# Squares of three norms summed by a matrix of ones onto all partitions, in place of column sums and diagonals

## The chip, the cores and the metric

The kernel runs on one core of a Trainium2 chip. The metric is the device time of one execution in microseconds (us), median of several runs.

## The reference

One inference step of a hybrid causal decoder trunk with two layers, for 1024 prompt positions and 8 x 8 sample positions (1088 tokens together), model width 1024, all in float32. What matters for the change are the norms:

```
def _rmsnorm(x, g):
    y = x * rsqrt(mean(x * x) + EPS);  return y * g
def _layernorm(x, g, b):
    xc = x - mean(x);  return xc * rsqrt(mean(xc * xc) + EPS) * g + b

for i in range(2):
    xn = rmsnorm(x, norm_mix_g[i]);  z = xn @ w_in[i]
    ...                              # branches a, c, d
    glu = z_cfa * sigmoid(z_cfb);  yb = causal_depthwise_conv31(glu)
    br_b = silu(layernorm(yb + bias, ln_g, ln_b))        # 256 channels
    mixed = sum over branches of sigmoid(z_gate) * (branch @ w_branch)
    x = x + mixed @ w_out[i]
    xn = rmsnorm(x, norm_ffn_g[i])
    x = x + (dense swiglu if i == 0 else top-2-of-8 swiglu experts)(xn)
    g = sigmoid(rmsnorm(x, norm_ple_g[i]) @ ple_w_gate[i])
    x = x + g * (p[i] @ ple_w_proj[i])
y = rmsnorm(x, final_norm_g)
```

## The kernel before

Activations lie transposed: channels on the 128 partitions (8 groups of 128 for the width 1024), the 1088 tokens along the free axis, cut into three BLOCKS of 384, 384 and 320. Every float32 product is made of three fast ones: weights and activations are split into a high and a low half (WHI and WLO, XHI and XLO), and `product` (L699) runs high x high, low x high, high x low for 8 groups, 24 matmuls into one bank. `column_unit` (L720) does this for one 128-column piece of a weight and the three blocks. Weights stream from HBM into WRAW (two buffers); ScalarE writes WHI (`convert`, L1278, with gains multiplied in first for some tiles, L1290) and VectorE writes WLO (L1703), about three units ahead of TensorE.

TensorE has eight PSUM banks: six (BANKS) for the products, taken in turn by `open_bank`, which waits until VectorE has read the bank of six before; and banks 6 and 7, taken in turn by `misc_bank` (L693) for sums, transposes and small products. `misc_bank` waits until the last use but one has been freed (semaphore misc_free, counted up by VectorE). The order of work on every engine is written out by hand: each engine runs its own program, a helper may be given a function `between`, run behind block 0 or 1 of a unit, and the engines meet in semaphores.

The gains of a norm are in the weights and its mean or root is applied after the product, as a factor per token, RSTD, of 128 equal rows (L1824, L2232). It comes about so:

1. the squares of all channels are added up to SQS (128 partitions x 1088 tokens), or SQB (two channel groups) in the layer norm;
2. `token_sums` (L726): per tile of 128 tokens a matmul with the squares as weights and one column of ones as data gives the sums with the tokens on the partitions, 128 x 9 numbers;
3. `norm_tokens` (L1740): VectorE copies these 9 columns to RTOK, ScalarE takes the root (`norm_sqrt`, L1317), VectorE the reciprocal (L1746);
4. `diagonals` (L1749): VectorE multiplies the identity by each column into T, 128 x 1088;
5. `spread` (L739): TensorE multiplies T by the matrix ONES, which puts each token's factor on all partitions; VectorE copies it to RSTD (`spread_rstd`, L1762), or multiplies YB by it (L2131) in the layer norm.

The order around the places of the change, before it:

- **Layer norm of the convolution branch** (both layers). TensorE runs one column unit, with the sums of YB over channels behind its block 0 (`channel_sums`, L923, already with the matrix of ones); then `token_sums(SQB)`; then a second column unit with `spread` behind block 0; then `gate_project("br_b")`, with `states_out` (L794: transposes of the pool branch's state, L803 and L807) behind its first block, and the branch products L754 to L756 behind its third. VectorE: subtracts the mean (L2115), squares (L2117), takes the first unit's products (L1878), then steps 3 to 5, then YB goes to ScalarE for Silu (L1441, L1442) and the high half (L1341), back for the low half (L1805), a WLO conversion, the second unit's products (L1878), and the copies that `states_out` needs (L1889).
- **Feed-forward norm** (layer 0). The first unit of the feed-forward has `stats` (= `token_sums(SQS)`) behind block 0 and `spread` behind block 1. VectorE, after step 5, fills ACC (L2223) and goes on with the products.
- **First embedding norm** (layer 0). The first block of `gate_project("p_ready")` is followed by the transposes of p (`p_columns`, L856) and `stats`, the second by `spread`. Behind the third stand the branch products, which also wait for the low half of their weights (PWL, `split_pw`, L1793), made by VectorE after step 5.

Of the kernel before, what the change touches and what calls it, by code (L numbers as in the profile page):

```python
# [138 lines left out]
def build(nc, A, O):  # L139
# [106 lines left out]
    def mo(name, shape, dt=F32):  # L246
# [85 lines left out]
        "xnew_ready", "y_full", "v_out", "par_ready", "rw_loaded", "nrs_loaded", "rtok_clear", "row_squares", "scale_ready", "ids_ready", "mask_ready", "list_ready", "rows_written", "squared", "summed", "sums_taken", "weights_ready", "spacer")}  # L332
# [347 lines left out]
    def _(pe):  # L680
# [53 lines left out]

        def stats():
            pe.wait_ge(S["sq_ready"], sq.take())
            token_sums(SQS)
# [109 lines left out]
        for l in range(DEPTH):  # L847
# [75 lines left out]
            def channel_sums():  # L923
                pe.wait_ge(S["yb_ready"], l + 1)
                for t0, n in BLOCKS:
                    b = misc_bank()
                    for k in range(2):
                        ins = pe.matmul(PS[:, b, 0:n], ONES[:], YB[:, k, t0:t0 + n], start=(k == 0), stop=(k == 1))
                    ins.then_inc(m.next(), 1)

            column_unit(XHI, XLO, between=(channel_sums,))
            pe.wait_ge(S["lnsq_ready"], l + 1)
            token_sums(SQB[:, 0, :], SQB[:, 1, :])
            column_unit(XHI, XLO, between=(spread,))
# [14 lines left out]
            if l == 0:  # L949
                hs = Count()  # L950

                def step(kind, g, first=False):
                    if kind == "GU":
                        for u in range(4):
                            if first and u == 0:
                                column_unit(XHI, XLO, splits=lambda j, k: W_FFN - 3 * KC + 3 * k + j + 1, between=(stats, spread))
# [294 lines left out]
            if l == 0:  # L1251
                last_down = W_FFN + 6 * FFN_GROUPS
                gate_project("p_ready", 1, P_SPLIT[0], splits=lambda j, k: last_down + 3 * k + j + 1,
                             between=(lambda: (p_columns([PTOK[:, i, :] for i in range(NT)]), stats()), spread))
# [17 lines left out]
    def _(act):  # L1272
# [44 lines left out]
        def norm_sqrt(count=D):  # L1317
            serve(lambda: act.activation(RTOK[:], RTOK[:], ACT.Sqrt, bias=EPSC[:], scale=1.0 / count))

# [80 lines left out]
        for l in range(DEPTH):  # L1400
# [35 lines left out]
            plain(1)  # L1436
            norm_sqrt(DB)
            plain(1)
            m.n += 1 + 3
# [24 lines left out]
            m.n += 1  # L1464
            norm_sqrt()
            if l == 0:
                m.n += 3
# [161 lines left out]
            if l == 0:  # L1629
                split_branch(PTS[0], P_SPLIT[0])  # L1630
                m.n += 6 + 1
            norm_sqrt()
            m.n += 3
# [57 lines left out]
    def _(dve):  # L1691
# [77 lines left out]
        def norm_rows():  # L1769
# [4 lines left out]
            v.sync()  # L1774

# [178 lines left out]
        for l in range(DEPTH):  # L1954
# [265 lines left out]
            if l == 0:  # L2220
                norm()
# [436 lines left out]
```

## Time and profile before

| | |
|---|---|
| Median of 3 runs | 5056.26 us (5048.07 to 5062.81) |
| Span of the profiled execution | 5055.9 us (its own time isn't given beside it) |
| Mean granted TensorE clock | 0.987 of full speed |
| Busy: TensorE, VectorE, ScalarE, GpSimd | 4935.7, 3231.2, 1745.1, 302.4 us |
| Share of the chain that ended last | TensorE 81%, no wait shown 9%, VectorE 5%, DMA 2%, ScalarE 1% |

Busy time is the time in which an engine runs instructions; PE is TensorE, PEld its weight loads, DVE VectorE, ACT ScalarE, POOL GpSimd. Matmuls are pipelined: a row's duration overlaps the next, so the distance from start to start tells what one costs. One float32 matmul stands as two records. The chain that ended last is followed back from the last instruction to what released it.

### The profile page before, as it was taken

To read this page: it belongs to the slowest core of one execution; us is meant where nothing else is said; L and a number is where in the kernel's file an instruction comes from. 1 tells how busy PE (TensorE), PEld (TensorE's weight loads), DVE (VectorE), ACT (ScalarE), POOL (GpSimd) and SP (SyncE) were. 2 spreads that over 40 slices of the span, in tenths; PEclk is the share of its full clock that TensorE was granted. 3 is DMA by queue.
4 is the path that set the end of the run, shared out by engine and by line. 5 is a ranking of instruction groups with operands and counts; after the bars stand their busy time and mean duration, and the time that the engine had idled before them with its cause. 6 is when DMAs were issued, how large, how long until landed. Compare 5 with 4: busy or idle time off the path is not lost.

```text
span 5055.9 us, 87486 instructions
## 1 busy us (share of the span) xinstructions
PE 4935.7 (98%) x33281; PEld 4878.9 (96%) x33282; DVE 3231.2 (64%) x5248; ACT 1745.1 (35%) x2666; POOL 302.4 (6%) x441
## 2 busy tenths in 40 slices
PE   8999999999999999999979999999999999999998
PEld 8999999999998999999979999999999999999988
DVE  4666656444546656766557777666667787876655
ACT  3323322111113433233234444333334444443333
POOL 2000002111112000000020000000000000000030
PEclk9999999999999999999989999999999999999999
DMA  3111111111111111111025554444446555554431
GB/s 107 45 47 41 42 39 42 51 41 41 50 42 44 42 46 52 48 41 42 30 90 197 178 178 165 157 141 161 153 150 197 188 194 186 197 192 153 142 134 43
DMA packets 397853, 521.94 MB, mean 103 GB/s; under 512 B 13192, under 2 KB 353654, under 8 KB 397512
## 3 DMA queue, kind: packets, MB, share of 16 engines
q1 hardware_dynamic: 358320, 459.63, 27.5%
q10 hardware_dynamic: 29272, 33.08, 1.9%
q0 software_dynamic: 9920, 24.85, 1.7%
q8 instruction: 193, 3.16, 0.3%
q14 instruction: 148, 1.21, 0.1%
HBM read 494.91 MB, written 22.60 MB: 102 GB/s over the span
## 4 chain that ended last, share of the span: by engine, by line
PE 81%; issue 9%; DVE 5%; DMA 2%; ACT 1%; DVEq 0%; POOL 0%; ACTq 0%; SPq 0%; POOLq 0%
PE PS L705 20%; PE PS L707 19%; PE PS L706 19%; PE PS L818 5%; PE PS L820 5%; PE PS L819 5%; PE PS L754 1%; PE PS L755 1%; PE PS L756 1%; DMA WRAW<-in_moe_w_gate 1%; DVE EACC L2509 1%; PE PS L1244 1%; DVE WLO L1703 1%; ACT WHI L1302 1%; DVE XSL L2458 0%
## 5 line engine op out<-in xcount | busy, mean ns | idle before, releaser
L1703 DVE TENSOR_TENSOR WLO<-WRAW,WHI 128x1024 fp32r<-128x1024 f32 x866 | 1060.0, 1225 | 417.9 <-ACT WHI L1302 298.3
L705 PE MATMUL PS<-XHI,WHI 128*128 128x384 f32 (+1 forms) x3648 | 1200.9, 329 | 14.4 <-DVE XLO L1960 8.3
L707 PE MATMUL PS<-XHI,WLO 128*128 128x384 f32 (+1 forms) x3648 | 1196.1, 328 | 0.0
L1302 ACT ACTIVATE WHI<-WRAW 128x1024 fp32r<-128x1024 f32 x866 | 899.3, 1051 | 858.8 <-PE PS L820 603.4
L706 PE MATMUL PS<-XLO,WHI 128*128 128x384 f32 (+1 forms) x3648 | 1195.2, 328 | 0.0
L705 PE MATMUL PS<-XSH,WHI 128*128 128x232 f32 (+6 forms) x3584 | 1059.1, 296 | 14.5 <-DVEq L2461 12.0
L707 PE MATMUL PS<-XSH,WLO 128*128 128x232 f32 (+6 forms) x3584 | 1055.6, 295 | 0.0
L706 PE MATMUL PS<-XSL,WHI 128*128 128x232 f32 (+6 forms) x3584 | 1054.1, 294 | 0.0
L705 PEld LDWEIGHTS PS<-XHI,WHI 128*128 128x128 f32 x3648 | 689.9, 189 | 16.6 <-issue 9.0
L705 PEld LDWEIGHTS PS<-XSH,WHI 128*128 128x128 f32 x3584 | 678.8, 189 | 16.6 <-DVEq L2461 13.6
L706 PEld LDWEIGHTS PS<-XLO,WHI 128*128 128x128 f32 x3648 | 689.7, 189 | 0.9
L707 PEld LDWEIGHTS PS<-XHI,WLO 128*128 128x128 f32 x3648 | 689.4, 189 | 0.0
L707 PEld LDWEIGHTS PS<-XSH,WLO 128*128 128x128 f32 x3584 | 679.0, 189 | 0.0
L706 PEld LDWEIGHTS PS<-XSL,WHI 128*128 128x128 f32 x3584 | 678.7, 189 | 0.0
L818 PE MATMUL PS<-EHI,WHI 128*128 128x232 f32 (+6 forms) x1792 | 532.0, 297 | 4.8 <-DVE EACC L2509 3.0
L820 PE MATMUL PS<-EHI,WLO 128*128 128x232 f32 (+6 forms) x1792 | 525.0, 293 | 0.0
L819 PE MATMUL PS<-ELO,WHI 128*128 128x232 f32 (+6 forms) x1792 | 524.5, 293 | 0.0
L2509 DVE TENSOR_TENSOR EACC<-PS,EACC 128x336 f32<-128x336 f32 x832 | 372.7, 499 | 43.1 <-PE PS L820 15.9
L818 PEld LDWEIGHTS PS<-EHI,WHI 128*128 128x128 f32 x1792 | 338.8, 189 | 7.2 <-DVE EACC L2509 3.8
L1346 ACT ACTIVATE T<-T 128x384 f32<-128x384 f32 (+1 forms) x240 | 121.9, 508 | 640.7 <-DVEq L1826 640.4
L819 PEld LDWEIGHTS PS<-ELO,WHI 128*128 128x128 f32 x1792 | 338.9, 189 | 0.0
L820 PEld LDWEIGHTS PS<-EHI,WLO 128*128 128x128 f32 x1792 | 338.8, 189 | 0.0
(408 smaller groups left out, 5810.6 us busy)
## 6 DMA issues: line engine op xcount, KB each, us to landing
WRAW<-in_moe_w_gate SPq DMA_DIRECT2D x112, 1024.0 KB, 5.0
WRAW<-in_moe_w_up SPq DMA_DIRECT2D x112, 1024.0 KB, 5.0
WRAW<-in_moe_w_down SPq DMA_DIRECT2D x112, 1024.0 KB, 4.9
WRAW<-in_w_in SPq DMA_DIRECT2D x48, 1024.0 KB, 5.2
WRAW<-in_ffn_w_gate SPq DMA_DIRECT2D x11, 1024.0 KB, 5.3
WRAW<-in_ffn_w_up SPq DMA_DIRECT2D x11, 1024.0 KB, 5.3
WRAW<-in_ffn_w_down SPq DMA_DIRECT2D x11, 1024.0 KB, 4.9
expert_rows<-YT ACTq DMA_DIRECT2D x18, 512.0 KB, 3.8
```

The lines of the kernel that those rows point to most:

```text
L705: pe.matmul(PS[:, bank, 0:n], wh, hi(k), start=(k == 0), stop=False)
L706: pe.matmul(PS[:, bank, 0:n], wh, lo(k), start=False, stop=False)
L707: ins = pe.matmul(PS[:, bank, 0:n], wl, hi(k), start=False, stop=(k == KC - 1))
L754: pe.matmul(PS[:, b, 0:n], wh[:, k, :], Y[0][:, k, t0:t0 + n], start=(k == 0), stop=False)
L755: pe.matmul(PS[:, b, 0:n], wh[:, k, :], Y[1][:, k, t0:t0 + n], start=False, stop=False)
L818: pe.matmul(PS[:, b, 0:n], WHI[s][:, d, :], hi[:, f, t0:t0 + n], start=(f == 0), stop=False)
L819: pe.matmul(PS[:, b, 0:n], WHI[s][:, d, :], lo[:, f, t0:t0 + n], start=False, stop=False)
L820: ins = pe.matmul(PS[:, b, 0:n], WLO[s][:, d, :], hi[:, f, t0:t0 + n], start=False, stop=(f == 1))
L1302: act.activation(WHI[halves.n % HL][:], raw_view(tile % RAW, half, kind), ACT.Copy).then_inc(halves.next(), 1)
L1346: serve(lambda: act.activation(t[:, 0:n], t[:, 0:n], ACT.Sigmoid))
L1703: v.do(dve.tensor_tensor(WLO[s][:], raw_view(conv.n // 2 % RAW, conv.n % 2, kind), WHI[s][:].bitcast(F32), ALU.subtract), conv)
L2509: v.do(dve.tensor_tensor(a, ps[:, 0:CAP], a, ALU.add), q)
```

## The change

The three norms no longer go through the 128 x 9 layout. `wide_sums` multiplies the squares by the matrix ONES with the tokens along the free axis, so each token's sum comes out on all 128 partitions. ScalarE takes the root out of the bank straight into RSTD (or into SQB, layer norm), block by block (`roots`), and VectorE takes the reciprocal in place and frees the bank (`reciprocal_roots`). The other norms keep the old way. In the layer norm the sums of the squares move from ahead of the second column unit to behind its block 0. In the embedding norm they move from behind block 0 to behind block 1. ScalarE's second weight conversion in the layer norm moves ahead of the root.

```diff
+        def wide_sums(*parts):
+            for t0, n in BLOCKS:
+                b = misc_bank()
+                for x, part in enumerate(parts):
+                    ins = pe.matmul(PS[:, b, 0:n], ONES[:], part[:, t0:t0 + n], start=(x == 0), stop=(x == len(parts) - 1))
+                ins.then_inc(m.next(), 1)
+        def wide_stats():
+            pe.wait_ge(S["sq_ready"], sq.take())
+            wide_sums(SQS)
...
             def channel_sums():
                 pe.wait_ge(S["yb_ready"], l + 1)
-                for t0, n in BLOCKS:
...
+                wide_sums(YB[:, 0, :], YB[:, 1, :])
+            def channel_squares():
+                pe.wait_ge(S["lnsq_ready"], l + 1)
+                wide_sums(SQB[:, 0, :], SQB[:, 1, :])
             column_unit(XHI, XLO, between=(channel_sums,))
-            pe.wait_ge(S["lnsq_ready"], l + 1)
-            token_sums(SQB[:, 0, :], SQB[:, 1, :])
-            column_unit(XHI, XLO, between=(spread,))
+            column_unit(XHI, XLO, between=(channel_squares,))
...
-                                column_unit(XHI, XLO, splits=..., between=(stats, spread))
+                                column_unit(XHI, XLO, splits=..., between=(wide_stats,))
...
-                             between=(lambda: (p_columns([PTOK[:, i, :] for i in range(NT)]), stats()), spread))
+                             between=(lambda: p_columns([PTOK[:, i, :] for i in range(NT)]), wide_stats))
...
+        def roots(dst, count):
+            for t0, n in BLOCKS:
+                act.wait_ge(S["misc_done"], m.n + 1)
+                act.activation(dst[:, t0:t0 + n], PS[:, 6 + m.n % 2, 0:n], ACT.Sqrt, bias=EPSC[:], scale=1.0 / count).then_inc(S["root_ready"], 1)
+                m.n += 1
...
-            plain(1)
-            norm_sqrt(DB)
-            plain(1)
-            m.n += 1 + 3
+            plain(2)
+            roots(SQB[:, 0, :], DB)
...
+        def reciprocal_roots(dst, then=lambda t0, n: None):
+            for t0, n in BLOCKS:
+                dve.wait_ge(S["root_ready"], rooted.take())
+                v.do(dve.reciprocal(dst[:, t0:t0 + n], dst[:, t0:t0 + n]), m)
+                v.sync()
+                then(t0, n)
...
-            norm_tokens()
-            diagonals()
-            for t0, n in BLOCKS:
-                ps = misc_ready()
-                for c in range(2):
-                    y = YB[:, c, t0:t0 + n]
-                    v.do(dve.tensor_tensor(y, y, ps[:, 0:n], ALU.mult), m if c else None)
+            def scale_channels(t0, n):
+                y = YB[:, :, t0:t0 + n]
+                v.do(dve.tensor_tensor(y, y, SQB[:, 0:1, t0:t0 + n].to_broadcast([P, 2, n]), ALU.mult))
+            reciprocal_roots(SQB[:, 0, :], scale_channels)
...
-                norm()
+                reciprocal_roots(RSTD)
```

In the feed-forward norm and the embedding norm of layer 0, ScalarE's `norm_sqrt()` becomes `roots(RSTD, D)` and VectorE's `norm()` becomes `reciprocal_roots(RSTD)`.

Two places show the order. First VectorE in the layer norm of layer 0, before, from the last of the first unit's products to the copies for the transposes:

```order
454 L1878 TENSOR_TENSOR ZP<-PS,RSTD 128x8x8
455 L1743 COPY RTOK<-PS 128x8
456 L1744 COPY RTOK<-PS 64x1
457 L1746 RECIPROCAL RTOK<-RTOK 128x9
458 L1755 TENSOR_TENSOR T_56<-IDF,RTOK 128x384
459 L1755 TENSOR_TENSOR T_57<-IDF,RTOK 128x384
460 L1755 TENSOR_TENSOR T_58<-IDF,RTOK 128x256
461 L1758 TENSOR_SCALAR T_58<-IDF,RTOK 128x64
462 L2131 TENSOR_TENSOR YB<-YB,PS 128x384 x4
463 L2131 TENSOR_TENSOR YB<-YB,PS 128x320 x2
464 L1805 TENSOR_TENSOR YBLO<-YB,YBHI 128x1088 x2
465 L1703 TENSOR_TENSOR WLO<-WRAW_52,WHI 128x1024
```

and with the change:

```order
454 L1907 TENSOR_TENSOR ZP<-PS,RSTD 128x8x8
455 L1801 RECIPROCAL SQB<-SQB 128x384
456 L2157 TENSOR_TENSOR YB<-YB,SQB 128x2x384
457 L1801 RECIPROCAL SQB<-SQB 128x384
458 L2157 TENSOR_TENSOR YB<-YB,SQB 128x2x384
459 L1801 RECIPROCAL SQB<-SQB 128x320
460 L2157 TENSOR_TENSOR YB<-YB,SQB 128x2x320
461 L1834 TENSOR_TENSOR YBLO<-YB,YBHI 128x1088 x2
462 L1722 TENSOR_TENSOR WLO<-WRAW_52,WHI 128x1024
```

Copies, the small reciprocal and the diagonals are gone; three reciprocals of whole blocks stand in their place, each ahead of its multiply.

Second ScalarE at the same place, before (L1302 writes WHI, L1318 is the root, L1441 and L1442 are Silu):

```order
153 L1302 ACTIVATE WHI<-WRAW_51 128x1024
154 L1318 ACT_TABLE_LOAD
155 L1318 ACTIVATE RTOK<-RTOK,EPSC 128x9
156 L1290 ACTIVATE WRAW_52<-WRAW_52,PAR 128x256 x8
157 L1302 ACTIVATE WHI<-WRAW_52 128x1024
158 L1441 ACT_TABLE_LOAD
159 L1441 ACTIVATE YB<-YB,PAR 128x1088
```

and with the change:

```order
153 L1312 ACTIVATE WHI<-WRAW_51 128x1024
154 L1300 ACTIVATE WRAW_52<-WRAW_52,PAR 128x256 x8
155 L1312 ACTIVATE WHI<-WRAW_52 128x1024
156 L1334 ACT_TABLE_LOAD
157 L1334 ACTIVATE SQB<-PS,EPSC 128x384 x2
158 L1334 ACTIVATE SQB<-PS,EPSC 128x320
159 L1456 ACT_TABLE_LOAD
```

The gains and the conversion of the next weight tile moved ahead of the table load and the roots, which now read the banks.

## Rows read from the trace of the kernel before

**Rows 1.** The page, busy time and share of the span by engine

```profile
PE 4935.7 (98%) x33281; PEld 4878.9 (96%) x33282; DVE 3231.2 (64%) x5248; ACT 1745.1 (35%) x2666; POOL 302.4 (6%) x441
```

**Rows 2.** The page, chain that ended last, share of the span by engine

```profile
PE 81%; issue 9%; DVE 5%; DMA 2%; ACT 1%; DVEq 0%; POOL 0%; ACTq 0%; SPq 0%; POOLq 0%
```

**Rows 3.** Windows, layer norm, layer 0: us; busy PE, PEld, DVE, ACT, POOL; clock; DMA

```profile
450.60:454.77 4.17, 4.17 (x27) 4.17 (x26) 0.99 (x2) 2.69 (x3) 0.00 (x0) 1.00 0.00 0
454.77:458.27 3.50, 3.50 (x13) 2.03 (x13) 1.98 (x4) 0.00 (x0) 0.00 (x0) 1.00 0.00 0
...
466.22:470.80 4.58, 4.58 (x39) 4.55 (x37) 0.56 (x2) 0.00 (x0) 0.00 (x0) 0.82 0.42 147
470.80:477.43 6.63, 6.63 (x25) 6.63 (x25) 1.96 (x7) 5.83 (x11) 0.00 (x0) 0.61 0.00 0
```

**Rows 4.** Timeline of TensorE, layer norm: start us, duration us, instruction [idle before, releaser]

```profile
479.35 0.81 PE L744 MATMUL PS<-T,ONES 128*128 128x320 f32 x2 [0.46 <-DVE YB L2131]
479.75 0.58 PE L705 MATMUL PS<-XHI,WHI 128*128 128x384 f32 x1
...
491.86 0.38 PE L803 MATMUL PS<-IDF,YP 128*120 128x128 f32 x2
...
2213.46 4.30 PE L732 MATMUL PS<-ONES,SQB 128*128 128x1 f32 x36
```

**Rows 5.** Windows, feed-forward norm and first embedding norm

```profile
833.53:835.51 1.98, 1.98 (x20) 1.95 (x19) 0.00 (x0) 0.00 (x0) 0.00 (x0) 1.00 0.01 4
...
839.79:841.65 1.86, 1.85 (x7) 0.90 (x7) 0.93 (x2) 0.00 (x0) 0.00 (x0) 1.00 0.00 0
...
1633.40:1637.10 3.70, 1.48 (x7) 1.08 (x5) 3.34 (x5) 1.58 (x3) 0.92 (x2) 0.50 0.00 0
...
1640.54:1644.34 3.80, 3.80 (x19) 3.77 (x18) 2.43 (x3) 3.06 (x3) 0.00 (x0) 0.50 0.02 4
1644.34:1651.27 6.93, 6.93 (x25) 6.93 (x25) 2.52 (x8) 3.17 (x5) 0.00 (x0) 0.58 0.06 19
...
1653.13:1656.88 3.75, 3.75 (x26) 3.67 (x25) 3.16 (x6) 0.42 (x1) 0.00 (x0) 1.00 0.00 0
```

**Rows 6.** Timeline of ScalarE, layer norm and feed-forward

```profile
450.96 1.04 ACT L1302 ACTIVATE WHI<-WRAW 128x1024 fp32r<-128x1024 f32 x1
452.02 1.28 ACT L1318 ACT_TABLE_LOAD   x1
...
854.14 0.53 ACT L1474 ACTIVATE GS<-GS 128x384 f32<-128x384 f32 x1 [15.58 <-DVEq L2234]
```

**Rows 7.** VectorE's reciprocals by line: duration ns min/median/max, first and last start

```profile
L1921 DVE RECIPROCAL WINV<-WIN x1: 165/165/165, 2.3 to 2.3; 128x2 f32<-128x2 f32 x1
...
L1746 DVE RECIPROCAL RTOK<-RTOK x8: 215/216/217, 471.6 to 5039.0; 128x9 f32<-128x9 f32 x8
...
L1927 DVE RECIPROCAL FIXT<-FIXT x1: 353/353/353, 2.9 to 2.9; 128x32 f32<-128x32 f32 x1
```

**Rows 8.** Timeline of VectorE, feed-forward norm and first embedding norm

```profile
842.62 9.71 DVE L2223 TENSOR_TENSOR ACC<-XHI,XLO 128x1088 f32<-128x1088 f32 x8
...
1653.57 0.49 DVE L1766 COPY RSTD<-PS 128x320 f32<-128x320 f32 x1 [0.25 <-PE PS L744]
1654.10 0.43 DVE L1793 TENSOR_TENSOR PWL<-PWR,PWH 128x256 fp32r<-128x256 f32 x1
```

**Rows 9.** Timeline of VectorE, layer norm, layer 0

```profile
456.26 1.02 DVE L2115 SCALAR_TENSOR_TENSOR YB<-PS,YB 128x384 f32<-128x384 f32 x2 [4.08 <-PE PS L928]
457.31 0.96 DVE L2117 TENSOR_TENSOR SQB<-YB 128x768 f32<-128x768 f32 x1
...
478.28 2.80 DVE L2131 TENSOR_TENSOR YB<-YB,PS 128x384 f32<-128x384 f32 x6 [4.87 <-PE PS L744]
...
490.21 0.35 DVE L1889 COPY YP<-ZP 128x120 f32<-128x120 f32 x2
```

**Rows 10.** Timeline of TensorE, first embedding norm

```profile
1632.64 0.44 PE L705 MATMUL PS<-XHI,WHI 128*128 128x384 f32 x1 [3.16 <-DVE XLO L1723]
```

More of the change, by code:

```diff
@@ L331, in build @@
         "counts_ready", "items_ready", "scattered", "xg_ready", "xg_used", "xs_ready", "ys_full", "ys_out", *(f"gathered{i}" for i in range(GATHERS)), "gather_used", "combined",
-        "xnew_ready", "y_full", "v_out", "par_ready", "rw_loaded", "nrs_loaded", "rtok_clear", "row_squares", "scale_ready", "ids_ready", "mask_ready", "list_ready", "rows_written", "squared", "summed", "sums_taken", "weights_ready", "spacer")}
+        "xnew_ready", "y_full", "v_out", "par_ready", "rw_loaded", "nrs_loaded", "rtok_clear", "row_squares", "scale_ready", "ids_ready", "mask_ready", "list_ready", "rows_written", "squared", "summed", "sums_taken", "weights_ready", "root_ready", "spacer")}
     mix_l = lambda l: [("col", l)] * 4 + [("col", l)] * 4 + [("col", l)] * 3 + [("col", l)] * 4 + [("col", l)] * 1 + [("col", l)] * 8
@@ L924, in channel_sums @@
                 pe.wait_ge(S["yb_ready"], l + 1)
-                for t0, n in BLOCKS:
[L926 to L929, printed above, removed]
+                wide_sums(YB[:, 0, :], YB[:, 1, :])
+            def channel_squares():
+                pe.wait_ge(S["lnsq_ready"], l + 1)
+                wide_sums(SQB[:, 0, :], SQB[:, 1, :])
             column_unit(XHI, XLO, between=(channel_sums,))
-            pe.wait_ge(S["lnsq_ready"], l + 1)
-            token_sums(SQB[:, 0, :], SQB[:, 1, :])
-            column_unit(XHI, XLO, between=(spread,))
+            column_unit(XHI, XLO, between=(channel_squares,))
             gate_project("br_b", l + 1, YB_SPLIT, between=(lambda: states_out(ZP, YP, PC),))
@@ L955, in step @@
                             if first and u == 0:
-                                column_unit(XHI, XLO, splits=lambda j, k: W_FFN - 3 * KC + 3 * k + j + 1, between=(stats, spread))
+                                column_unit(XHI, XLO, splits=lambda j, k: W_FFN - 3 * KC + 3 * k + j + 1, between=(wide_stats,))
                             else:
@@ L1463, in _ @@
                 q.n += 3
-            m.n += 1
-            norm_sqrt()
             if l == 0:
-                m.n += 3
+                roots(RSTD, D)
+            else:
+                m.n += 1
+                norm_sqrt()
+            if l == 0:
                 def step(kind, g, last=False):
@@ L1630, in _ @@
                 split_branch(PTS[0], P_SPLIT[0])
-                m.n += 6 + 1
-            norm_sqrt()
-            m.n += 3
+                m.n += 6
+                roots(RSTD, D)
+            else:
+                norm_sqrt()
+                m.n += 3
             split_pw()
@@ L1774, in norm_rows @@
             v.sync()
+        rooted = Count()
+        def reciprocal_roots(dst, then=lambda t0, n: None):
[4 more added lines that the diff above has]
+                then(t0, n)
         def norm():
@@ L2574, in _ @@
                 p_columns(PTS[0], P_SPLIT[0])
-            norm()
+                reciprocal_roots(RSTD)
+            else:
+                norm()
             split_pw()
```

## The prediction

> **What bounds the kernel now.** I read the busy table first. TensorE is busy for 98% of the span and VectorE for 64% [rows 1]. The chain that ended last runs through TensorE for 81% and through VectorE for 5% [rows 2]. So work taken from TensorE's queue shortens the kernel, as long as nobody is late for it afterwards, and VectorE's own work counts only where TensorE waits for its end. The edit touches four places: the layer norm of the convolution branch (once per layer), the feed-forward norm and the first embedding norm. For each I read TensorE's windows, then its timeline, then VectorE's.
>
> In the layer norm of layer 0 the sums over single columns hold TensorE for 4.58 us. The 24 matmuls behind them take 6.63 us at a mean granted clock of 0.61 of full speed, where the same block takes 4.17 us at 1.00. The spreading of the diagonals then takes 2.32 us (477.43 to 479.75), 0.46 us of it a wait [rows 3, 4]. In layer 1 they begin 1747.2 us later, at 2213.46 [rows 4], and I take the same price. The feed-forward norm pays 1.98 us and 1.86 us with the clock at 1.00. The embedding norm pays 3.80 us for the same sums at half clock, then a block of 6.93 us, then again 1.86 us (1651.27 to 1653.13) [rows 5].
>
> **What is removed from TensorE.** Layer norm: 4.58 + 2.32 = 6.90 us, and the 6.63 - 4.17 = 2.46 us that the block behind loses at the lower clock. Feed-forward: 1.98 + 1.86 = 3.84 us. Embedding: 3.80 + 1.86 = 5.66 us. What is put in: the wide sums of the squares are the instructions of the channel sums, 3.50 us for 2 x 1088 columns [rows 3], 1.6 ns a column. That is 3.50 us in the layer norm (three blocks of 1.24, 1.24 and 1.03) and about 1.8 us, the price of the spreading, in the two others. On TensorE alone the change would give 2 x (6.90 + 2.46 - 3.50) + 2.0 + 3.9 = 17.6 us. I expect nearly all of it to be lost to a wait.
>
> **The new chain.** A bank of sums is freed only when VectorE's reciprocal of its block has ended, and there are two such banks. The third block's sums therefore wait for sums, root and reciprocal of the first. The root is a ScalarE pass over 128x384; no row has Sqrt in that size, and I take 0.53 us from the pass of that size there is [rows 6]. Its table load comes ahead of it: ScalarE's second weight conversion, moved in front, is released when TensorE ends the first column unit at 466.22, and 1.04 us of conversion and 1.28 us of load [rows 6] end at 468.6, before the sums do. The reciprocal goes from 9 columns on 128 partitions to 384, 384 and 320. Three rows bear on it: 165 ns for 2 columns, 216 for 9, 353 for 32 [rows 7]. From 2 to 32 that is 6.27 ns a column, where VectorE's copy of 128x320 needs 0.49 us, 1.5 ns a column [rows 8]. Going on in a line, 384 columns take 0.165 + 382 x 0.00627 = 2.56 us and 320 take 2.16 us. The lower bound is the streaming price of other VectorE work, 0.56 us. The upper bound is the steepest step, 2 to 9 columns, 7.1 ns a column: 2.89 and 2.44 us. I take 2.56, since 32 columns are the size nearest to 384.
>
> **Layer norm.** The squares' sums stand behind the first block of the next unit, so they begin at 466.22 + 4.17 = 470.39. VectorE reached the first block of the channel sums 1.49 us after their start (456.26 against 454.77) [rows 3, 9]. So ScalarE starts at 471.88 and VectorE at 472.5. Then VectorE has 2.56, a multiply of both channel halves 128x768 at 0.96 [rows 9], 2.56, 0.96, 2.16 and 0.8 for 128x640 (0.96 scaled), with about 0.3 us between: it ends near 482.8. Before, its multiplies ended at 478.28 + 2.80 = 481.08 [rows 9]. TensorE: the third sums start near 475.1 after 2.2 us of waiting and end at 476.1. The rest of the unit and the first gate block, 12.1 us before (479.75 to 491.86 [rows 4]), bring it to 488.2, where the transposes of the pool state (L803) stand. These need the copies at L1889, which ended at 490.56 [rows 9] and now come 1.7 us later, at 492.3. TensorE, which passed that place at 491.86 without a wait [rows 4], now stands there for 4.1 us and goes on at 492.3. What it saved is gone, and 0.5 us more. Behind it all VectorE and ScalarE work shifts by the same 0.5 us.
>
> **Feed-forward norm.** From the start of the sums: first bank after 0.62 us, root from 0.85 to 1.38, reciprocal from 1.5 to 4.06, third sums from 4.15 to 4.7. TensorE stands for 2.9 us. 4.7 against 3.84 is 0.8 us more. VectorE has the scale at 833.53 + 8.8 = 842.3, and its next work, the adds of L2223, began at 842.62 [rows 8]; so nothing later moves.
>
> **Embedding norm.** The column sums behind the transposes go, so the block of 6.93 us starts at 1640.54 [rows 5]. I leave its time, since the clock is already down ahead of it. The sums start at 1647.47 and end at 1652.2, the last block of 3.75 us at 1655.9. The first branch product also waits for the low half of its weights (L1793). VectorE makes it after the reciprocals: before at 1654.10 for 0.43 us [rows 8], now from 1647.47 + 8.8 = 1656.3, ready near 1656.9. TensorE passed there at 1656.88 [rows 5]: plus 0.1 us.
>
> **The clock.** After 3.16 us without work at 1629.5 TensorE's granted clock was 0.50 in the stretch from 1633.40, that is 1.2 GHz in place of 2.4 [rows 5, 10]. A lower clock cost the next block 2.46 us in one place and 6.93 - 4.17 = 2.76 us in the other [rows 3, 5]. The new waits are 4.1 us (layer norm) and 2.9 us (feed-forward). I put 2.0 us behind each layer norm, since part of the slow time falls into the wait itself, and 1.5 us behind the feed-forward norm, whose wait is shorter than any I saw followed by a fall. The bounds are 0 and 2.76 us each. In the embedding norm the wait for L1793 takes up about 1 us and I put nothing.
>
> Sum: 2 x (0.5 + 2.0) + (0.8 + 1.5) + 0.1 = 7.4 us. The profiled execution has a span of 5055.9 us, and the median of the three runs is 0.4 us above that, so I take the sum against the median: 5056.3 + 7.4 = 5063.7 us. The other norms (both mixing norms, layer 1's feed-forward and embedding, the last one) are not touched. The four edits have no other cost: ScalarE passes of 0.53 us lie in its idle time, and it is busy for 35% [rows 1].
>
> **The rivals.** Bound for all: 0.3% is 15.2 us, about what a measurement of this kernel tells from no change (the three runs lie 14.7 us apart).
>
> A. Reciprocals run at streaming speed. VectorE's layer norm chain then ends at 472.5 + 3 x 0.56 + 2.75 + 0.2 = 477.1, the copies at 486.6, and TensorE, there at 486.3, saves 5.2 us a layer. Feed-forward: third sums from 2.15 us on, 1.1 us saved. Embedding: 3.0 us saved. Total -14.5 us, 5041.8, within some 4 us either way. For it speaks that a short instruction has a fixed part; against it that 9 to 32 columns still cost 6.0 ns each [rows 7]. 0.14.
>
> B. The waits come as worked out, but the clock stays up: 2 x 0.5 + 0.8 + 0.1 = +1.9 us, 5058.2. For it: the sums on both sides of the 2.9 us wait are full matmuls, which held the clock at 1.00 in the channel sums [rows 3]. Against it: the 4.1 us wait is longer than the 3.16 us one. 0.22.
>
> C. Slower: the reciprocal's line is steeper, and TensorE's wait becomes the long one everywhere. At 7.1 ns a column each reciprocal costs 0.33 us more, so the layer norm +0.9 each, feed-forward +0.3, embedding +0.9; and every wait costs the full 2.76 us of clock. 2 x (0.5 + 0.9 + 2.76) + (0.8 + 0.3 + 2.76) + (0.1 + 0.9 + 2.76) = +15.9 us, 5072.2. It decides from 384 columns at about 2.9 us on, since VectorE is then later than any slack TensorE has. Against it: 9 to 32 columns are less steep, not steeper. 0.18. The rule of the Trainium skill's page "VectorE: DVE Perf Modes" above would go still further this way.
>
> **How the numbers follow.** Forecast 0.46, A 0.14, B 0.22, C 0.18. The range takes in forecast, B and most of C: 5048 to 5073. A is left out but for its edge. Faster by over 0.3% (below 5041.1): two thirds of A, since the fast chain may also keep the clock up, 0.09. Slower (above 5071.4): two thirds of C, 0.12, and 0.01 of the forecast, 0.13. Within: 0.78.
>
> **What would show it.** Right: reciprocals of 128x384 near 2.56 us; TensorE waiting some 2.2 us ahead of the third sums and some 4 us ahead of L803's transposes in both layers, and 2.9 us in the feed-forward norm; no lower clock right behind the squares' sums, but one behind the wait at the transposes. Wrong: reciprocals well under 1.5 us, or the transposes reached after VectorE's copies have ended; then TensorE's 17.6 us are real. The time is also wrong if code that merely shifted changes TensorE's loops, of which the trace of before tells nothing.

## The result and the profile after

| | before | changed |
|---|---|---|
| Median | 5057.1 us (5047.31 to 5062.81, 15 runs) | 5064.6 us (5061.45 to 5069.7, 15 runs) |
| Ratio of the times | | 1.0016, 95% interval 1.0008 to 1.0023 |
| Profiled execution: time, span | span 5055.9 us | 5061.68, 5060.1 us |
| Mean granted TensorE clock | 0.987 | 0.987 |

The change costs 7.5 us (4.0 to 11.6 by the interval), 0.16%. The page of the changed kernel, busy time by engine and the chain that ended last, answers to [rows 1, 2]:

```profile
PE 4925.6 (97%) x33185; PEld 4866.1 (96%) x33186; DVE 3249.1 (64%) x5220; ACT 1750.9 (35%) x2674; POOL 302.1 (6%) x441
...
PE 89%; DVE 5%; issue 2%; ACT 1%; DMA 1%; DVEq 0%; SPq 0%; ACTq 0%; POOL 0%; POOLq 0%
```

TensorE has 10.1 us less to do and the kernel is not faster: the work saved has turned into waits. The three largest new ones, in TensorE's waits (us in total, times, longest), are below; before, the same places had one wait of 0.46 us per layer norm [rows 4]:

```profile
PE PS L740 <- DVE RSTD L1801: 5.3, 2, 2.7
...
PE PS L740 <- DVE SQB L1801: 4.1, 2, 2.0
PE PS L815 <- DVE YP L1918: 4.0, 2, 2.0
```

L740 are the wide sums, L1801 the reciprocals, L815 the transposes of the pool state (L803 before). The two instructions that make the new chain, by line (duration ns min/median/max, first and last start):

```profile
L1801 DVE RECIPROCAL SQB<-SQB x6: 2144/2544/2553, 471.2 to 2228.7; 128x384 f32<-128x384 f32 x4, 128x320 f32<-128x320 f32 x2
...
L1334 ACT ACTIVATE SQB<-PS,EPSC x6: 527/580/580, 470.5 to 2226.5; 128x384 f32<-128x384 f32 x4, 128x320 f32<-128x320 f32 x2
```

384 columns take 2.55 us, 320 take 2.14 us. From the 353 ns of 32 columns [rows 7] to 384 that is 6.2 ns a column, nearly the 6.27 ns that [rows 7] gave from 2 to 32. The layer norm of layer 0 on TensorE, then on VectorE, against [rows 3, 4, 9]:

```profile
469.04 2.74 PE L740 MATMUL PS<-SQB,ONES 128*128 128x384 f32 x8
473.82 2.50 PE L740 MATMUL PS<-SQB,ONES 128*128 128x320 f32 x4 [2.04 <-DVE SQB L1801]
...
490.68 0.55 PE L815 MATMUL PS<-IDF,YP 128*120 128x128 f32 x2 [2.03 <-DVE YP L1918]
```

```profile
471.21 2.55 DVE L1801 RECIPROCAL SQB<-SQB 128x384 f32<-128x384 f32 x1 [5.61 <-ACT SQB L1334]
...
490.27 0.35 DVE L1918 COPY YP<-ZP 128x120 f32<-128x120 f32 x2
```

TensorE stands before the third sums until the first reciprocal has freed the bank, and again before the transposes until VectorE's copies, which end the chain of reciprocals, multiplies, Silu, low half and one unit's products. To compare kernels I use four stretches on TensorE's timeline: the layer norm from the first channel sums to the first product of branch b (454.77 to 500.00 us before), the feed-forward norm from the first block's start to the second unit's, and the embedding norm from the first transposes of p to the second unit of the gate. The window of the layer norm stretch, layer 0 (columns as in [rows 3]; before: 45.23 us at a clock of 0.92):

```profile
453.40:500.43 47.03, 42.96 (x221) 38.77 (x221) 28.99 (x41) 14.15 (x18) 0.00 (x0) 0.93 0.13 40
```

TensorE is busy for less of it (42.96 us against 44.77) and VectorE for more (28.99 against 22.65). In the feed-forward norm, and in the embedding norm up to the first branch product, TensorE's timeline has:

```profile
837.98 0.81 PE L740 MATMUL PS<-SQS,ONES 128*128 128x320 f32 x2 [2.69 <-DVE RSTD L1801]
...
1652.04 0.81 PE L740 MATMUL PS<-SQS,ONES 128*128 128x320 f32 x2 [2.61 <-DVE RSTD L1801]
1657.38 0.41 PE L766 MATMUL PS<-PTHI,PWH 128*128 128x384 f32 x1 [1.01 <-issue]
```

The wait of 1.01 us at L766 has no releaser in the profile ("issue"). The branch product also needs the low half of its weights (PWL), which VectorE makes right behind the last reciprocal and which ends 0.16 us before TensorE goes on (e1 has the same distance, 1654.88 to 1655.04):

```profile
1654.61 2.15 DVE L1801 RECIPROCAL RSTD<-RSTD 128x320 f32<-128x320 f32 x1
1656.80 0.42 DVE L1822 TENSOR_TENSOR PWL<-PWR,PWH 128x256 fp32r<-128x256 f32 x1
```

### The profile page after: what moved, and what is told of

It reads as the page before. It is cut to its first block, busy times and chain, and to the rows that moved or that the text cites. A ratio compares the mean times of both kernels' runs of the same rounds, so it can differ in the third digit from the quotient of the medians.

```text
span 5060.1 us, 87266 instructions
## 1 busy us (share of the span) xinstructions
PE 4925.6 (97%) x33185; PEld 4866.1 (96%) x33186; DVE 3249.1 (64%) x5220; ACT 1750.9 (35%) x2674; POOL 302.1 (6%) x441
## 4 chain that ended last, share of the span: by engine, by line
PE 89%; DVE 5%; issue 2%; ACT 1%; DMA 1%; DVEq 0%; SPq 0%; ACTq 0%; POOL 0%; POOLq 0%
PE PS L705 21%; PE PS L707 21%; PE PS L706 21%; PE PS L830 6%; PE PS L831 6%; PE PS L832 6%; PE PS L766 1%; PE PS L767 1%; PE PS L768 1%; PE PS L1254 1%; DVE EACC L2537 0%; DVE XSL L2486 0%; DVE WLO L1722 0%; ACT WHI L1312 0%; DMA WRAW<-in_moe_w_gate 0%
## 5 line engine op out<-in xcount | busy, mean ns | idle before, releaser
L705 PE MATMUL PS<-XHI,WHI 128*128 128x384 f32 (+1 forms) x3648 | 1201.2, 329 | 14.3 <-DVE XLO L1989 8.2
L705 PE MATMUL PS<-XSH,WHI 128*128 128x232 f32 (+6 forms) x3584 | 1058.9, 295 | 14.6 <-DVEq L2489 10.8
L705 PEld LDWEIGHTS PS<-XHI,WHI 128*128 128x128 f32 x3648 | 690.0, 189 | 16.9 <-issue 9.3
L705 PEld LDWEIGHTS PS<-XSH,WHI 128*128 128x128 f32 x3584 | 679.3, 190 | 16.7 <-DVEq L2489 15.0
```

The costliest lines, as they stand in the source:

```text
L705: pe.matmul(PS[:, bank, 0:n], wh, hi(k), start=(k == 0), stop=False)
```

## The experiments

Each kernel is an edit of the changed one, unless said otherwise. The stretches in us (two values: layers 0 and 1); "before" and "changed" have two traces each, from the first profile and from e9 and e10 (one execution each: 5053.8 and 5066.2 us):

| kernel | layer norm | feed-forward | embedding | median us, ratio to before on that chip (95%) |
|---|---|---|---|---|
| before | 45.23, 45.21; 43.76, 45.21 | 16.07; 16.07 | 26.45; 25.79 | |
| changed | 47.03, 47.00; 46.93, 46.88 | 18.21; 18.10 | 24.22; 25.99 | 5064.6, 1.0016 (1.0008 to 1.0023) |
| e1 bank freed by root | 46.87, 47.08 | 13.99 | 28.50 | 5059.2, 1.0008 (0.9999 to 1.0018) |
| e2 squares' sums early | 44.32, 44.33 | 18.21 | 24.34 | 5059.1, 1.0011 (1.0002 to 1.0020) |
| e3 reciprocals twice | 53.66, 53.86 | 20.94 | 35.27 | 5088.9 (2 runs), 1.0068 (1.0049 to 1.0086) |
| e4 no reciprocals, early | 40.05, 40.03 | 13.99 | 23.01 | 5043.8, 0.9981 (0.9972 to 0.9990) |
| e5 early, roots first | 43.14, 43.16 | 18.24 | 26.26 | 5054.3, 1.0002 (0.9993 to 1.0012) |
| e6 no reciprocals, late | 43.77, 43.82 | 13.99 | 22.19 | 5050.7, 0.9994 (0.9984 to 1.0003) |
| e7 layer norm only | 47.06, 47.03 | 16.05 | 25.88 | 5061.1, 1.0018 (1.0008 to 1.0027) |
| e8 all three | 41.28, 41.26 | 13.99 | 24.01 | 5045.9, 0.9986 (0.9976 to 0.9996) |
| e11 before + 7 on ScalarE | 43.72, 43.67 | 16.08 | 26.49 | 5052.5, 1.0000 (0.9990 to 1.0009) |
| e12 before + 15 on ScalarE | 42.13, 45.24 | 16.02 | 25.82 | 5048.8, 0.9988 (0.9979 to 0.9998) |

### e1: the bank is freed by the root

```
-   ... ACT.Sqrt, ...).then_inc(S["root_ready"], 1)
+   ... ACT.Sqrt, ...).then_inc(S["misc_free"], 1)
-   dve.wait_ge(S["root_ready"], rooted.take())
-   v.do(dve.reciprocal(dst[:, t0:t0 + n], dst[:, t0:t0 + n]), m)
+   dve.wait_ge(S["misc_free"], m.take())
+   v.do(dve.reciprocal(dst[:, t0:t0 + n], dst[:, t0:t0 + n]))
```

> Changed kernel, but ScalarE's root frees the bank of the sums, not VectorE's reciprocal. Stretches of TensorE, before / changed: layer norm from the first channel sums to the first branch product 45.23 / 47.03 us; feed-forward unit with the norm 16.07 / 18.21 us; embedding norm from the second batch of transposes to the first branch product 19.72 / 17.76 us. Theory (the third sums wait for the reciprocal only because it frees the bank; the ends of the layer norm and the embedding norm hang on VectorE's chain of reciprocals): feed-forward 14.2 us (2.5 of wait and 1.5 of slow clock gone); layer norm unchanged at 47 us, its wait at the transposes grown from 2.0 to 4 to 6 us; embedding unchanged near 17.8 us, its wait for the weights' low half grown from 1.0 to near 4 us. In all 4 us less than changed, 5060.6 us. Rival (the wait ahead of the third sums is what costs, everywhere): all four stretches shorter by 2.0 to 2.7 us, 9 to 14 us less, 5051 to 5056 us.

TensorE's timeline of the layer norm and of the embedding norm:

```profile
468.73 3.82 PE L740 MATMUL PS<-SQB,ONES 128*128 128x384 f32 x12
490.37 0.68 PE L815 MATMUL PS<-IDF,YP 128*120 128x128 f32 x2 [5.96 <-DVE YP L1918]
...
1655.04 0.66 PE L766 MATMUL PS<-PTHI,PWH 128*128 128x384 f32 x1 [3.60 <-issue]
```

No third sums wait, and the layer norm takes as long as with the wait: the gain has gone into the wait at the transposes. It is 5.96 us, against 3.66 in the changed kernel's second trace (e10), where the clock too stayed up until there, and 2.03 in the first. From the first channel sums to the transposes it is 37.28 us in e1 (453.09 to 490.37), 37.28 and 37.27 in the two traces of the changed kernel. In the embedding norm the third sums' 2.61 us reappear at the branch product (3.60 us for 1.01), 9.40 us behind the sums' start as in the changed kernel (9.41); that stretch is 28.50 us, longer than was expected, with a granted clock of 0.70 in it. Only the feed-forward norm, where VectorE has time, keeps the gain: 13.99 us. So freeing the bank earlier pays only where nothing of VectorE's is due soon after.

### e2: the squares' sums ahead of the second unit

```
-   column_unit(XHI, XLO, between=(channel_squares,))
+   channel_squares()
+   column_unit(XHI, XLO)
```

> Changed kernel, but the sums of the squares stand ahead of block 0 of the second column unit, where the column sums stood, and not behind it. Theory (the layer norm's end is set by VectorE's chain, which starts with these sums): each layer norm stretch falls by the 4.2 us by which the chain starts earlier, from 47.0 to 42.8 us, and to 41.5 if the clock recovers sooner; TensorE still waits some 1.5 us at the transposes. 8.4 to 11 us less than changed, 5054 to 5056 us. Rival (the sums' own work and the clock behind their wait cost the time, not the chain): the same work in another place, stretches within 1 us of 47.0, 5064 us.

```profile
466.51 2.74 PE L740 MATMUL PS<-SQB,ONES 128*128 128x384 f32 x8
472.43 1.95 PE L740 MATMUL PS<-SQB,ONES 128*128 128x320 f32 x4 [3.18 <-DVE SQB L1802]
```

The stretch fell by 2.7 us where 4.2 were expected (and by no more than 1 by the rival), the wait at the transposes is gone, and the wait for the third sums grew to 3.18 us, on TensorE's timeline above. ScalarE's timeline has the reason: conversion and table load, which the change put ahead of the roots, now end behind the sums, and the first root starts 2.63 us after them (469.14 - 466.51) instead of 1.46:

```profile
466.77 1.06 ACT L1313 ACTIVATE WHI<-WRAW 128x1024 fp32r<-128x1024 f32 x1 [11.27 <-PE PS L707]
467.84 1.28 ACT L1335 ACT_TABLE_LOAD   x1
469.14 1.05 ACT L1335 ACTIVATE SQB<-PS,EPSC 128x384 f32<-128x384 f32 x2
```

### e3: every new reciprocal twice

```
+   v.do(dve.reciprocal(T[1][:, 0:n], dst[:, t0:t0 + n]))
    v.do(dve.reciprocal(dst[:, t0:t0 + n], dst[:, t0:t0 + n]), m)
```

The added result is read by nobody.

> Changed kernel with every reciprocal of a block done twice on VectorE (once more ahead of it, into a scratch tile). Theory: a layer norm grows by all three, 2 x 2.55 + 2.14 = 7.2 us, to 54.3 us; feed-forward only by the one that frees the first bank, 2.55 us, to 20.8 us; embedding by 7.2 us, to 25 us; in all 24 us more than changed, 5089 us. Rival (reciprocals are partly hidden: TensorE has slack at the transposes or at the weights' low half): less than 5 us in a layer norm, under 15 us in all.

```profile
475.95 2.16 PE L740 MATMUL PS<-SQB,ONES 128*128 128x320 f32 x4 [4.45 <-DVE SQB L1802]
```

The third sums are later by one reciprocal (a wait of 4.45 us for 2.04), and the layer norms by 6.6 and 6.9 us, nearly the three reciprocals' 7.2 us: TensorE has hardly any slack there. The feed-forward norm grew by 2.7 us, one reciprocal, as expected; the embedding norm by 11.1 us, more than its three, at a granted clock of 0.66 (0.83 in the changed kernel's first trace). In total 24.3 us more than the changed kernel for 12 reciprocals of 29 us, by the median of only two executions.

### e4: logarithm and exponential on ScalarE, no reciprocals, sums early

```
-   ... ACT.Sqrt, bias=EPSC[:], scale=1.0 / count).then_inc(S["root_ready"], 1)
+   ... ACT.Ln, bias=EPSC[:], scale=1.0 / count).then_inc(S["misc_free"], 1)
+   act.wait_ge(S["misc_free"], m.n)
+   for t0, n in BLOCKS:
+       act.activation(dst[...], dst[...], ACT.Exp, scale=-0.5).then_inc(S["root_ready"], 1)
```

and the edit of e2; VectorE's reciprocal is gone.

> Changed kernel without any reciprocal: ScalarE makes 1 / root as exp(-0.5 ln(mean + eps)), three Ln passes out of the banks, which they free, then three Exp passes in place; sums of the layer norm's squares ahead of block 0 of the second unit. Theory (TensorE's own saving was real and is only eaten by the reciprocals): layer norm 45.23 - 6.90 - 2.46 + 3.50 = 39.4 us with no wait at the transposes; feed-forward 14.2 us; embedding near 16 us, bounded by one table load and three passes ahead of the weights' low half. About 17 us less than before, 5040 us. Rival (another wait or the lower clock takes the place): layer norm no better than 42 us, 5048 us or more.

```profile
464.55 2.74 PE L740 MATMUL PS<-SQB,ONES 128*128 128x384 f32 x8
467.81 1.34 PE L740 MATMUL PS<-SQB,ONES 128*128 128x320 f32 x4 [0.52 <-ACT SQB L1335]
```

No wait at the transposes, granted clock 1.00 in both layer norms, and stretches near the expected ones (40.05 us for 39.4, 13.99 for 14.2). ScalarE loads a table again between logarithms and exponentials, which the changed kernel does not need:

```profile
469.74 1.28 ACT L1339 ACT_TABLE_LOAD   x1
471.03 1.30 ACT L1339 ACTIVATE SQB<-SQB 128x384 f32<-128x384 f32 x3
```

This is the fastest kernel here, but the total missed its forecast: about 17 us under before were expected, and the medians differ by 10.0 us (5.1 to 14.2 by the interval), 0.19%. What the four stretches give is 13.7 us, against their means over the traces in the old form (before twice, e11 and e12: 44.27, 16.06 and 26.14 us).

### e5: as e2, with the roots ahead of the weight conversion

```
-   plain(2)
+   plain(1)
    roots(SQB[:, 0, :], DB)
+   plain(1)
```

> Both layer norms as in the run with the squares' sums moved ahead of the second unit, but ScalarE converts the next weight tile behind the three roots, as the kernel before had it, so that the table load falls into its idle time. Theory (in the early kernel the roots, not the reciprocals, were late: the first root began 2.63 us after the sums, against 1.46 us in the changed kernel, because conversion and table load stood ahead of it): the first root begins 1.5 us after the sums' start, the wait ahead of the third sums falls from 3.18 to 2.0 us, there is still no wait at the transposes, and the layer norm stretch goes from 44.3 to 43.1 us in each layer; total about 2.3 us under the early kernel's 5059.1. Rival (that stretch is set by the three reciprocals alone): wait stays near 3.2 us and the stretch at 44.3 us. A second rival (the conversion, now later, makes VectorE late with the low half of the weights): a new wait of TensorE at the branch products or the next gate unit, stretch at 44 us or more.

```profile
471.95 1.34 PE L740 MATMUL PS<-SQB,ONES 128*128 128x320 f32 x4 [2.04 <-DVE SQB L1803]
```

As the theory had it: wait 2.04 us, stretch 43.14 us, and no new wait behind it, which the second rival had named. The total fell by 4.8 us where 2.3 us were expected; medians out of two different comparisons don't resolve that.

### e6: as e4, but with the sums where the change put them

> The reciprocals are gone (ScalarE computes exp(-ln(x)/2), three logarithms out of the banks, then three exponentials), but in the layer norm the squares' sums stay behind block 0 of the second unit, where the change put them. It splits the gain of the earlier run with both steps (40.05 us per layer norm against 47.0). Theory: no wait ahead of the third sums; VectorE's multiplies end 9.1 us after the sums' start (3.5 sums, 1.0 to the last logarithm, 1.3 table load, then exponentials at the pace of the multiplies, 3 x 0.96) in place of 12.1 us; TensorE still reaches the transposes before VectorE's copies, and waits some 2.9 us; the stretch is 43.9 us, feed-forward 13.99 us, embedding 16 to 16.5 us. Total 12 us under the changed kernel, near 5052. Rival (the reciprocals are the whole cause, the place of the sums matters little): no wait at the transposes and 40.0 to 40.5 us per layer norm, total near 5045.

```profile
469.00 3.82 PE L740 MATMUL PS<-SQB,ONES 128*128 128x384 f32 x12
487.44 0.43 PE L815 MATMUL PS<-IDF,YP 128*120 128x128 f32 x2 [2.75 <-DVE YP L1920]
```

Of the 7.0 us that e4 gains on the changed kernel in a layer norm, 3.2 us come from the reciprocals (and the clock that their waits cost), and 3.8 us from the earlier place. Taken in the other order it is nearly the same: 3.9 us for the earlier place with the roots first (changed kernel to e5), then 3.1 us for the reciprocals (e5 to e4). The rival, reciprocals alone, falls.

### e7: only the layer norms changed

The feed-forward norm and the first embedding norm keep `stats`, `norm` and `spread`.

> Only the two layer norms are changed; the feed-forward norm and the first embedding norm keep column sums, diagonals and spreading as in the kernel before. Theory (the parts add up): layer norm 47.0 us each (+1.8 each), feed-forward 16.07 us as before, in the embedding norm the block behind the column sums again 6.9 us long; total 3.6 us over the kernel before. Rival (what is lost in the layer norm is made up by slack further on, or the changed time comes from elsewhere in the program): within 1 us of the kernel before, or 6 us and more over it.

TensorE's two timelines at the transposes, layers 0 and 1:

```profile
489.30 0.65 PE L815 MATMUL PS<-IDF,YP 128*120 128x128 f32 x2 [3.64 <-DVE YP L1914]
...
2239.06 0.43 PE L815 MATMUL PS<-IDF,YP 128*120 128x128 f32 x2 [2.07 <-DVE YP L1914]
```

The stretches add up as expected. They also show that the wait at the transposes is not a fixed size: with a granted clock of 0.96 in the stretch it is 3.64 us, with 0.93 it is 2.07 us, and the stretch is 47.06 and 47.03 us. VectorE sets the wait's end; what a clock that falls ahead of the wait costs is taken out of the wait. The median, however, is 8.7 us over before (4.0 to 13.6 by the interval), where the stretches of the first traces gave 3.6: by the total the rival of 6 us and more is nearer. e9 to e12 look for the reason.

### e8: three edits that leave the reciprocals on VectorE

Those of e1 and e5, and in the embedding norm the branch's weights ahead of roots and reciprocals:

```
+   split_pw()
    roots(RSTD, D)
...
+   split_pw()
    reciprocal_roots(RSTD)
```

> The reciprocals stay on VectorE. Three edits to the changed kernel: the bank is freed by the root, the layer norm's squares are summed ahead of the second unit with the weight conversion behind the roots, and in the embedding norm both engines make the branch's weights ahead of roots and reciprocals. Theory (each reciprocal's price stays, but TensorE meets it only where VectorE's products are next needed): no wait ahead of third sums anywhere; layer norm 42.6 us with a wait of about 1.7 us at the transposes (5.96 us when only the bank was freed early); feed-forward 13.99 us; in the embedding norm no wait for the weights (3.60 us before), and from the sums' start to the first matmul of the second unit 10.8 us in place of 14.97; total near 5046, 13 us under the run with the bank alone. Rival (VectorE's chain is the bound in all places, so its end sets TensorE whatever is rearranged): layer norm at 44.3 us or more, embedding 14 us or more from the sums to the second unit, total at 5055 or above.

```profile
485.59 0.44 PE L815 MATMUL PS<-IDF,YP 128*120 128x128 f32 x2 [1.80 <-DVE YP L1921]
...
1638.34 2.29 PE L740 MATMUL PS<-SQS,ONES 128*128 128x384 f32 x6
...
1649.00 0.41 PE L705 MATMUL PS<-XHI,WHI 128*128 128x384 f32 x1 [1.90 <-DVE T L1856]
```

Wait at the transposes 1.80 us (1.7 expected), sums to second unit 10.66 us (10.8 expected), total 5045.9 us (5046 expected); the layer norm, 41.28 us, is below the 42.6, at a granted clock of 1.00. In its stretches the new idea beats the old one with its reciprocals, once TensorE hardly meets them: 10.2 us in all four, against the same means. The medians differ by 6.4 us (2.0 to 12.1 by the interval), and a difference of that size does not prove it alone, since e12 below has 5.0 us without any gain of this kind.

### e9 and e10: second traces of before and of the changed kernel

> The kernel before, unedited, for a second trace of it. In the traces so far the changed places account for +3.8 us of the changed kernel, and the same places for +3.5 us in the kernel with only the layer norms changed, while the medians rose by 7.5 and 8.7 us. In every changed trace TensorE also waits 1.5 us at about 3505 us for the low half of an expert's weights, where the first trace of before has no wait, and the stretch behind the second layer norm (2808.7 us in before) is 2805 to 2816 us long. Theory (that stretch varies from execution to execution and has nothing to do with the edits): this trace has a stretch of 2810 us or more, or the wait at 3505 us. Rival (the edits cost some 3 to 5 us there, by shifted code): 2809 us or less again, and no wait at 3505 us. The layer norm stretches stay at 45.2 us and the feed-forward norm at 16.1 us in both.

> The changed kernel, unedited, for a second trace of it. Both theories: layer norm stretches 47.0 us, feed-forward 18.2 us, third sums late by 2.0, 2.0, 2.7 and 2.6 us. Theory (the stretch behind the second layer norm varies from execution to execution): it differs from the first trace's 2809.1 us by 2 us or more, in either direction. Rival (fixed cost of the edits): within 1 us of it.

Windows of before, second trace, the two layer norms (columns as in [rows 3]):

```profile
451.96:495.72 43.76, 43.29 (x251) 40.61 (x251) 22.66 (x45) 13.74 (x19) 0.00 (x0) 0.96 0.12 33
2198.44:2243.65 45.21, 44.74 (x252) 42.07 (x251) 22.66 (x45) 13.72 (x19) 0.00 (x0) 0.92 0.11 32
```

Before, TensorE sets the pace of this stretch, so that the clock shows in it: 45.2 us at 0.92, 43.8 at 0.96, and 42.13 at 1.00 in e12 (453.41 to 495.54). In the changed kernel it is 46.9 to 47.0 us in both traces. Where the clock falls differs between them. Windows behind the third sums' wait and behind the wait at the transposes, first the first trace, then the second:

```profile
473.82:475.65 1.83, 1.83 (x4) 1.24 (x5) 1.83 (x2) 0.00 (x0) 0.00 (x0) 0.50 0.00 0
490.68:500.43 9.75, 9.75 (x52) 9.62 (x53) 5.24 (x9) 3.80 (x6) 0.00 (x0) 0.82 0.28 82
...
474.84:491.71 16.87, 13.21 (x76) 12.58 (x76) 12.72 (x14) 6.41 (x6) 0.00 (x0) 0.99 0.00 1
491.71:501.37 9.66, 9.66 (x53) 9.53 (x54) 5.02 (x9) 3.58 (x5) 0.00 (x0) 0.83 0.25 75
```

The same wait of 2.04 us ended at half clock in the first trace and left the clock up in the second, which then waits 3.66 us at the transposes. Behind the transposes the clock falls in both. The second trace has 25.99 us in the embedding norm.

Behind the second layer norm, before takes 2808.7 and 2808.5 us, the changed kernel 2809.1 and 2812.2. No edit of any kernel here touches that part of the program, and yet it takes 2800.7 us in e12, 2805.3 in e4, 2814.8 in e6 and 2815.6 in e8. By what was expected of them, the trace of before speaks for a fixed cost of the edits and that of the changed kernel for variation; so neither is ruled out. One part is the same in both traces of each kernel. At the first expert of layer 1 ScalarE stands still without a releaser, here in the second trace of before and in the changed kernel:

```profile
3493.05 1.28 ACT L1302 ACT_TABLE_LOAD   x1 [6.42 <-issue]
```

```profile
3502.41 1.28 ACT L1312 ACT_TABLE_LOAD   x1 [8.25 <-issue]
```

It is 6.4 us in both traces of before and 8.3 us in both of the changed kernel, in which TensorE then waits 1.4 to 1.5 us (L705, for the low half of the weights); before, it doesn't. In e3 ScalarE stands still for 8.25 us too, and TensorE does not wait.

### e11 and e12: before with more ScalarE code

```
+   for i in range(7):      # 15 in e12
+       act.activation(PAD[:, 1 + i:2 + i], EPSC[:], ACT.Copy)
```

> The kernel before, with seven more ScalarE instructions and nothing else: copies of one column into spare columns that nobody reads, at a place of layer 0 (the feed-forward norm) where ScalarE has time. In both traces of before, and in the kernel with only the layer norms changed (four ScalarE instructions more), ScalarE stands still for 6.42 to 6.54 us with no releaser at the first expert of layer 1, near 3493 to 3499 us; in all kernels with eight or more additional ones it stands for 8.2 to 9.7 us, and TensorE then waits 1.4 to 3.0 us for the low half of the weights, where before it had no such wait. Theory (the longer stand is a matter of where ScalarE's code lies, not of what the change computes): with seven more instructions the stand is 8 us or more and TensorE's wait is 1.4 us or more; the layer norms and the two other norms take what they took before. Rival (it comes with the changed norms themselves, through their timing): 6.4 to 6.5 us and no wait. Total 1.5 us over before by the theory, 0 by the rival; both are less than the timing can tell.

> As the run with seven more instructions, with fifteen. Theory: ScalarE's stand at the first expert again differs from the 6.4 us of before, at 8 to 10 us, with a TensorE wait behind it of 1.4 to 3 us; the value need not grow with the count. Rival: 6.4 to 6.5 us and no wait.

Seven: 6.46 us and no wait, against the theory. Fifteen, ScalarE's timeline:

```profile
3491.62 1.28 ACT L1303 ACT_TABLE_LOAD   x1 [7.20 <-issue]
```

7.20 us and a wait of 0.7 us: ScalarE's stand does change with code that has nothing to do with the norms, but by less than the 8 to 10 us expected, so neither run shows that shifted code makes the changed kernel's 8.3 us. Behind the second layer norm e12's trace takes 2800.7 us (5043.2 - 2242.52), 8 us less than before, and its median is 5.0 us below before (0.12%, by the interval 0.02 to 0.21%). So added instructions that compute nothing may move this kernel by not much less than the change did.

## Why the prediction held

Predicted 5063.7 us, measured 5064.6. The mechanism was the one described: TensorE's saving became waits for VectorE's reciprocals. That the total agrees within 0.9 us is partly luck, since the measured difference of 7.5 us is only known to some 4 us either way, and the spans of the two pairs of traces differ by 4.2 and 12.4 us. By its steps:

- **Reciprocal** 2.56 and 2.16 us: measured 2.55 and 2.14. The line through the short rows held out to 384 columns. Two bounds were slightly off: the copy's 1.5 ns a column gives 0.59 us for the lower one, not 0.56, and the step from 2 to 9 columns is 7.3 ns by the medians [rows 7], not 7.1; neither changes the forecast.
- **Third sums** late by 2.2 us (layer norm) and 2.9 (feed-forward): 2.04 and 2.69, in the embedding norm 2.61. The root, 0.58 us out of the bank, was taken as 0.53.
- **Wait at the transposes** 4.1 us: 2.03 in the first trace, 3.66 in the second. The forecast kept the clock up until that wait, as the second trace has it. In the first it fell earlier, at the end of the third sums' wait, and TensorE came later by as much.
- **Layer norm** +0.5 and +2.0 us: from the channel sums to the transposes +0.2 (37.28 against 37.09), behind them +1.6 (9.75 against 8.14). In all it is +1.8 against the first traces, and against the mean of eight layer norms in the old form (44.27 us over before, e9, e11 and e12) it is +2.7 for the changed kernel's 46.96. The step that read the price of the old form took the clock of one trace, 0.92, as part of the kernel; it is in four of those eight; three have 0.96 and one 1.00.
- **Feed-forward** +2.3 us: +2.1.
- **Embedding** +0.1 us: -2.2 between the first traces, where the clock came back up at 0.84 in the block ahead of the sums (4.97 us against 6.93 [rows 5]), and +0.2 between the second ones. As means of four and of two, 26.14 and 25.11, -1.0 us. The sums' start to the branch product took 9.41 us in the first trace, as worked out. In the second the block ahead took 5.96 us, and the one behind the third sums' wait 5.31 us at a clock of 0.68; the forecast had kept the first at 6.93 and the second at 3.75, with no clock cost, and the two misses cancel in part.

The sum of the means is 2 x 2.7 + 2.1 - 1.0 = 6.5 us, for a predicted 7.4 and a measured 7.5 (4.0 to 11.6). The prediction named shifted code as a thing that could make it wrong. The wait at the first expert adds some 1.5 us; whether shifted code causes it stays open, and so does what is added elsewhere: e7 has no such wait, and its median is still 3.4 us above what its stretches give against the means of before (8.7 against 2 x 2.8 - 0.3 = 5.3 us), within its interval.

**Rivals.** A, streaming reciprocals: refuted by the 2.55 us. B, clock stays up: refuted by the granted clock of 0.91 in the feed-forward stretch (829.65 to 847.86), which had 1.00 before (829.34 to 845.41), and of 0.82 and 0.83 behind the wait at the transposes. C, a steeper line: refuted by the 2.55 us, where it needed about 2.9.

What was forecast but is shown only by the experiments: that VectorE sets the end of the layer norm. e1 took one wait away and the transposes began no earlier; e3 lengthened the chain and TensorE followed almost fully; e4, e5, e6 and e8 shortened it, or began it earlier, and TensorE followed until it was itself the slower. This is shown for the stretches. For the total, the 1 us between 6.5 and 7.5 is within the interval.

## What to carry to other kernels

Moving a small-layout step (9 columns) to a full layout (1088 columns) saves TensorE the way through the small layout but multiplies any operation whose time goes by columns; price that one first, here 7.2 us of reciprocals for 0.2. Then ask who is next late: a wait that goes only pays if the engine behind it has time, and starting the chain 4.2 us earlier (e6 to e4, 3.8 us gained) gave more than taking the reciprocals out of it (changed kernel to e6, 3.2 us). Before a difference of 0.1% in the total is put down to an edit, take two traces of each kernel, and one of a kernel with idle instructions added.

## What was not expected of the hardware

- With fifteen one-column ScalarE copies added the kernel was 0.12% faster (0.02 to 0.21%), and ScalarE's stand at the first expert took 6.42 to 9.70 us in kernels that differ in a few instructions ahead of it (9.70 in e8, with 3.0 us of waiting on TensorE), while it agreed within 0.03 us between two executions of the same kernel. What decides it was not found.
- The layer norm stretch of before has a granted clock of 0.92 or 0.96 in two executions of the same kernel, and 1.00 in e12, where it holds the same instructions: 45.2, 43.8 and 42.1 us. A wait of 2.04 us ahead of the third sums ended at a clock of 0.50 in the changed kernel's first trace and left it up in the second; in e8 a wait of 1.80 us at the transposes leaves it at 1.00.
- A reciprocal of 128x384 takes 2.55 us, and the second of two in a row on the same input (e3) 2.49 to 2.50.
